# Attention's value product in high and low parts: the probabilities' low part on VectorE ahead of the next maximum

## What is computed

```
logits = einsum('bnqhgd,bnkhd->bnhgqk', qb, kb) * HEAD_DIM ** -0.5
logits = where(valid, logits, -1e30)
probs = softmax(concatenate([logits, sink_col], -1), -1)[..., :-1]
out = einsum('bnhgqk,bnkhd->bnqhgd', probs, vb)
```

## Time and profile before

| | us |
|---|---|
| median of 3 runs | 950.02 (949.94 to 950.05) |
| span of the profiled execution, first to last instruction | 948.2 |
| TensorE busy | 928.1 (98%) |
| TensorE weight loads | 800.5 (84%) |
| VectorE busy | 724.2 (76%) |
| ScalarE busy | 576.6 (61%) |

### The profile page before, as it was taken

The page is one execution under the profiler, slowest core; times in us unless marked ns, Lnnn a source line. Parts: engine busy times, 40 slices in busy tenths (PEclk is TensorE's granted clock), DMA queues, the critical chain, the costliest instruction groups (busy, mean ns, idle before and its releaser), DMA issues.

```text
span 948.2 us, 12500 instructions
## 1 busy us (share of the span) xinstructions
PE 928.1 (98%) x5068; PEld 800.5 (84%) x5068; DVE 724.2 (76%) x971; ACT 576.6 (61%) x730; POOL 1.4 (0%) x9
## 2 busy tenths in 40 slices
PE   4999999999999999999999999999999999999996
PEld 3898888988888888888889889888888888888885
DVE  5887898787867867767867688888878676866755
ACT  4578889764356644555345889887435564545540
POOL 0000000000000000000000000000000000000000
PEclk9999999999999999999999999999999999999998
DMA  9546444584485655566453544456756656555621
GB/s 330 159 160 200 135 156 156 185 303 166 156 266 183 200 195 178 194 201 207 157 162 122 204 159 157 132 179 192 261 177 216 229 185 203 189 179 196 202 90 45
DMA packets 118457, 174.62 MB, mean 184 GB/s; under 512 B 3968, under 2 KB 78976, under 8 KB 117888
## 3 DMA queue, kind: packets, MB, share of 16 engines
q1 hardware_dynamic: 118256, 173.79, 55.1%
q10 hardware_dynamic: 144, 0.03, 0.0%
HBM read 172.76 MB, written 1.05 MB: 183 GB/s over the span
## 4 chain that ended last, share of the span: by engine, by line
PE 97%; DVE 1%; DMA 1%; ACT 0%; SPq 0%; issue 0%; DVEq 0%
PE ring L541 16%; PE ring L543 16%; PE ring L542 16%; PE ring L594 9%; PE ring L590 9%; PE ring L593 5%; PE ring L591 5%; PE misc L543 5%; PE misc L541 5%; PE misc L542 4%; PE misc L771 2%; PE misc L809 1%; PE misc L829 1%; PE ring L714 1%; DMA sb_hb<-in_w_in_dram 1%; PE ring L725 1%
## 5 line engine op out<-in xcount | busy, mean ns | idle before, releaser
L1245 DVE TENSOR_TENSOR sb_w_lo<-sb_raw,sb_w_hi 128x2048 fp32r<-128x2048 f32 x138 | 294.7, 2148 | 67.5 <-ACT sb_w_hi L925 67.4
L925 ACT CAST sb_w_hi<-sb_raw 128x2048 fp32r<-128x2048 f32 x138 | 246.2, 1795 | 16.1 <-DMA sb_raw<-in_w_proj_rnn_dram 3.9
L541 PE MATMUL ring<-sb_w_hi,sb_x_both 128*128 128x512 f32 x272 | 108.1, 397 | 0.0
L594 PE MATMUL ring<-sb_x_both,sb_w_hi 128*128 128x512 f32 x272 | 107.6, 396 | 0.0
L590 PE MATMUL ring<-sb_x_both,sb_w_hi 128*128 128x512 f32 x272 | 107.5, 395 | 0.0
L543 PE MATMUL ring<-sb_w_hi,sb_x_both 128*128 128x512 f32 x272 | 106.1, 390 | 0.0
L542 PE MATMUL ring<-sb_w_lo,sb_x_both 128*128 128x512 f32 x272 | 106.0, 390 | 0.0
L593 PE MATMUL ring<-sb_x_both,sb_w_lo 128*128 128x256 f32 x272 | 75.7, 278 | 0.0
L591 PE MATMUL ring<-sb_x_both,sb_w_lo 128*128 128x256 f32 x272 | 75.4, 277 | 0.0
L541 PE MATMUL ring<-sb_x_both,sb_w_hi 128*128 128x256 f32 x256 | 73.0, 285 | 0.0
L543 PE MATMUL ring<-sb_x_both,sb_w_lo 128*128 128x256 f32 x256 | 72.4, 283 | 0.0
(11 more groups left out here) (223 smaller groups left out, 2085.8 us busy)
## 6 DMA issues: line engine op xcount, KB each, us to landing
sb_raw<-in_w_in_dram SPq DMA_DIRECT2D x40, 1024.0 KB, 5.2
sb_raw<-in_w_up_dram SPq DMA_DIRECT2D x34, 1024.0 KB, 5.2
sb_raw<-in_w_down_dram SPq DMA_DIRECT2D x18, 1024.0 KB, 4.9
sb_raw<-in_w_proj_attn_dram SPq DMA_DIRECT2D x8, 1024.0 KB, 5.0
sb_raw<-in_w_proj_rnn_dram SPq DMA_DIRECT2D x8, 1024.0 KB, 5.1
sb_hb<-in_w_up_dram SPq DMA_DIRECT2D x8, 1024.0 KB, 5.2
sb_raw<-in_w_out_dram SPq DMA_DIRECT2D x6, 1024.0 KB, 6.0
sb_raw<-in_w_ple_gate_dram SPq DMA_DIRECT2D x6, 1024.0 KB, 5.7
```

The source lines that it names most:

```text
L541: nc.tensor.matmul(dst, lhs[0], rhs[0], start=first, stop=False)
L594: last = nc.tensor.matmul(bank_of(*key), hi[:, cols], x_both[:, k + 1], start=False, stop=k + 2 == KT)
L925: nc.scalar.copy(hi_at[home][:, at], raw_at[home][:, at]).then_inc(s_hi_part, 1)
L1245: nc.vector.tensor_tensor(lo_at[home][:, 0:size], raw_at[home][:, 0:size], hi_at[home][:, 0:size].bitcast(F32), ALU.subtract).then_inc(s_s ...
```

## The change

The value product becomes three float32r products. For that both operands get a high and a low part:

- `v_hi` is a ScalarE copy of the values, once a layer, behind the last copy of turned keys in unit `ga0` (i = 2). `v_lo` is a VectorE subtraction, once a layer, in unit i = 3.
- `p_hi` is what `probs_back` writes, in the place of `pT`. `p_lo` is a VectorE subtraction that reads misc banks 2 and 3, in units 3 to 6, behind the taps and ahead of `softmax_max`.
- The new tiles lie on memory that is free by then: `v_hi` on the end of `qk`, `v_lo` on `v` itself, `p_lo` on the front of `qkT`, `p_hi` on `pT`. For the place of `p_lo`, round 0 also waits for the scores of round 1.
- `mix_values` waits for `v_lo` and `p_lo` and issues six float32r matmuls of 512 columns in the place of two float32 ones.

```
@@ -282,9 +282,12 @@
 
         h = sb("h", [P, TT, D])
         lnp = sb("lnp", [P, 2, D])
-        qk = sb("qk", [P, TT, QK_HEADS, HEAD_DIM])
-        v = sb("v", [P, TT, KV_HEADS, HEAD_DIM])
-        qkT = sb("qkT", [P, QK_HEADS, SEQ])
+        qk, at = sb_at("qk", [P, TT, QK_HEADS, HEAD_DIM])
+        v_hi = again("v_hi", [P, TT, KV_HEADS, HEAD_DIM], F32R, at + 4 * KT * SEQ)
+        v, at = sb_at("v", [P, TT, KV_HEADS, HEAD_DIM])
+        v_lo = again("v_lo", [P, TT, KV_HEADS, HEAD_DIM], F32R, at)
+        qkT, at = sb_at("qkT", [P, QK_HEADS, SEQ])
+        p_lo = again("p_lo", [P, TT, GROUP, P], F32R, at)
         yg = qk[:, :, :, :].rearrange("p t h d -> p (t h d)")[:, 0:KT * SEQ].rearrange(
             "p (k s) -> p k s", k=KT)
         hf = lnp[:, :, :].rearrange("p i (k s) -> p (i k) s", s=SEQ)
@@ -294,7 +297,8 @@
         ga = sb("ga", [P, TT, D])
         gr = xT[:, :, :].rearrange("p (t a) s -> p t (a s)", t=TT)
         soft = sb("soft", [P, GROUP, SEQ])
-        pT = sb("pT", [P, TT, GROUP, P])
+        pT, at = sb_at("pT", [P, TT, GROUP, P])
+        p_hi = again("p_hi", [P, TT, GROUP, P], F32R, at)
         scan_in, at = sb_at("scan_in", [P, 2, 4, SEQ])
         decay_a, root_m = scan_in[:, 0], scan_in[:, 1]
         scan_hi = again("scan_hi", [P, 2 * 4 * SEQ], F32R, at)
@@ -824,10 +831,11 @@
 
             def mix_values(l, r):
 
-                pe.wait_ge(s_probs_back, value("probs_back", l, r + 1))
+                pe.wait_ge(s_v_ready, value("v_ready", l, 1))
+                pe.wait_ge(s_probs_lo, value("probs_lo", l, r + 1))
                 for kb in range(TT):
-                    last = nc.tensor.matmul(misc[:, 2, :], v[:, kb, r // TT, :], pT[:, kb, :, :],
-                                            start=kb == 0, stop=kb == TT - 1)
+                    last = three(misc[:, 2, :], [x[:, kb, r // TT, :] for x in (v_hi, v_lo)],
+                                 [p_hi[:, kb, :, :], p_lo[:, kb, :, :]], kb == 0, kb == TT - 1)
                 last.then_inc(s_mixed, 1)
 
 
@@ -1027,7 +1035,7 @@
 
             def probs_back(l, r):
                 act.wait_ge(s_probs_turned, value("probs_turned", l, r + 1))
-                nc.scalar.copy(pT[:, :, :, :].rearrange("p a g t -> p (a g t)"),
+                nc.scalar.copy(p_hi[:, :, :, :].rearrange("p a g t -> p (a g t)"),
                                misc[:, 2:4, :].rearrange("p a n -> p (a n)")).then_inc(s_probs_back, 1)
 
             def attn_out(l, r):
@@ -1165,6 +1173,9 @@
                         conv_base(l, i + 2)
                     if name == "ga0":
                         qk_copies(l, [4])
+                        all_emptied(act, l, [("kv", t) for t in range(TT)])
+                        nc.scalar.copy(v_hi[:, :, :, :].rearrange("p t h d -> p (t h d)"),
+                                       v[:, :, :, :].rearrange("p t h d -> p (t h d)")).then_inc(s_v_hi, 1)
                     if 3 <= i <= 6:
                         probs_back(l, i - 3)
                     if i % 2 == 1:
@@ -1447,6 +1458,23 @@
                     last = nc.vector.tensor_scalar(soft[:, i, :], soft[:, i, :], sm[:, 5, i:i + 1], None, ALU.mult)
                 last.then_inc(s_probs, 1)
 
+            def v_low(l):
+                dve.wait_ge(s_v_hi, value("v_hi", l, 1))
+                nc.vector.tensor_tensor(v_lo[:, :, :, :].rearrange("p t h d -> p (t h d)"),
+                                        v[:, :, :, :].rearrange("p t h d -> p (t h d)"),
+                                        v_hi[:, :, :, :].rearrange("p t h d -> p (t h d)").bitcast(F32),
+                                        ALU.subtract).then_inc(s_v_ready, 1)
+
+            def probs_low(l, r):
+
+                dve.wait_ge(s_probs_back, value("probs_back", l, r + 1))
+                if r == 0:
+                    dve.wait_ge(s_scores, value("scores", l, TT))
+                nc.vector.tensor_tensor(p_lo[:, :, :, :].rearrange("p a g t -> p (a g t)"),
+                                        misc[:, 2:4, :].rearrange("p a n -> p (a n)"),
+                                        p_hi[:, :, :, :].rearrange("p a g t -> p (a g t)").bitcast(F32),
+                                        ALU.subtract).then_inc(s_probs_lo, 1)
+
             def attn_out(l, r):
                 g, b = divmod(r, TT)
                 at = (slice(None), slice(GROUP * g, GROUP * (g + 1)), slice(b * P, (b + 1) * P))
@@ -1630,6 +1658,10 @@
                     split_to(l, name, 1)
                     if i + 2 < 2 * RNN_BLOCKS:
                         conv(l, i + 2)
+                    if i == 3:
+                        v_low(l)
+                    if 3 <= i <= 6:
+                        probs_low(l, i - 3)
                     if 2 <= i <= 5:
                         softmax_max(l, i - 2)
                     if name == "kv":
```

More of the change, by code:

```diff
@@ L238 @@
 PER = dict(
-    ln_step=2 * TT * LN_STEPS, ln_norm=4 * TT, x_turned=3 * 4, x_hi=3 * 4, x_ready=3 * 4,
+    probs_lo=ROUNDS, v_ready=1, v_hi=1, ln_step=2 * TT * LN_STEPS, ln_norm=4 * TT, x_turned=3 * 4, x_hi=3 * 4, x_ready=3 * 4,
     rope_step=6, qk_turned=5, qk_ready=5,
@@ L353, in hybrid_encoder @@
         s_probs_back = sem("probs_back")
+        s_probs_lo = sem("probs_lo")
+        s_v_hi = sem("v_hi")
+        s_v_ready = sem("v_ready")
         s_mixed = sem("mixed")
```

## The result

The changed kernel takes 951.78 us (median of 16 runs, 951.58 to 953.16) against 950.16 us for the kernel before (16 runs, 949.93 to 951.33): ratio 1.0017, 95% interval 1.0010 to 1.0023, so 1.6 us slower. The forecast was 951.6.

The account below looks back on a forecast made before the run. TensorE, busy 928.1 of 948.2 us, was taken as the bound. Per layer 1.44 us saved against 2.25 waited gave +0.8, twice +1.6: median 951.6 us, 0.17% slower, range 949.4 to 954.0.

Parts of the forecast that it names:

- What TensorE saves: Value products in each round: six float32r at 0.227 us replace 1.72 us, saving 0.36 per round, 2.9 in all.
- Rival 3: Value products much cheaper than 0.227 us, at 0.12, but TensorE mostly waits for VectorE's slots: 949.8 us; chance 0.06.
- What VectorE pays: Added subtractions on VectorE: 1.73 us in round 0, 1.13 in other rounds; VectorE busy 11.1 us more.
- Round 1's wait: TensorE's value products in round 1 wait 0.71 us for VectorE's low part of the probabilities.
- The sum: Per layer 1.44 us saved and 2.25 waited: +0.8, twice +1.6, median 951.6 us.
- the case's own range: Forecast case with its bounds for saving, restart and turnings: +0.1 to +1.6 us a layer, 950.2 to 953.2 us.
- ScalarE's cover: ScalarE's copy of the values, near 0.6 us, costs nothing in the 2.74 us idle before the first exponentials.
- Rival 1: VectorE's slot comes 1.3 us earlier, so low parts are in time and the saving arrives whole: 947.1 us; chance 0.06.
- Rival 2: VectorE's backlog never drains, every round waits like round 0: 957.8 us, or half, 954 to 955; chance 0.14.
- Where the backlog drains: VectorE's backlog falls to some 1.5 us by round 2, in its 1.06 us idle before 146.57.
- Rival 4: TensorE's clock falls in the new waits, costing microseconds each time; chance 0.04 together with anything unseen.
- The cover of the weight splits: Weights' low parts are made three pieces ahead on VectorE, so a backlog up to 2.6 us there costs nothing.

Follow-up runs that it names:

- e1: The changed kernel with six float32r products on the high parts alone, no low parts made or waited for: 947.43 us, ratio 0.997.
- e2: The changed kernel with VectorE's subtractions kept, but the value product float32 and waiting only for ScalarE's copy: 952.57 us, ratio 1.0027.
- e4: The changed kernel with both low-part subtractions moved ahead of the convolution's six taps on VectorE: 951.82 us, ratio 1.0018.
- e8: The changed kernel with the subtractions behind the next round's maximum instead of ahead of it: 964.29 us, ratio 1.0143.
- e7: The changed kernel with values' low part earlier, probabilities' ahead of the taps, and two weight splits moved behind the attention output's low part: 949.83 us.
- e10: e7 with round 3's probabilities' low part also moved ahead of a weight split: 948.76 us, ratio 0.9986.
- e9: The changed kernel with values' low part earlier, probabilities' low part in two halves, first three products behind the first half: 951.07 us, ratio 1.0010.

## Why the prediction was right

The mechanism is the one forecast: TensorE waits for VectorE's low part in rounds 0 and 1, is late enough in rounds 2 and 3 not to wait, and what it loses is a little more than what the products save. Round by round in layer 0. Lags are counted from the first turning, which is 0.28 us later than before.

| step | forecast | measured |
|---|---|---|
| round 0: wait | 1.34 | 1.35 |
| lag at the next turning | 1.08 | 129.91 - 128.50 - 0.28 = 1.13 |
| round 1: wait | 0.71 | 0.51 |
| lag at round 2 | 1.43 | 156.38 - 154.71 - 0.28 = 1.39 |
| rounds 2 and 3: wait | none | none |
| lag behind round 3 | 0.8 | 174.19 - 173.10 - 0.28 = 0.81 |

(173.10 is the first gate product of the kernel before, taken from its record's end, 173.38, less 0.28.)

- **What TensorE saves.** 0.227 a product was right: 0.23 in the rows after, 0.34 us a round in e1 against 0.36 forecast. Rival 3, the cheap product, is out.
- **What VectorE pays.** The low part ends and the products start where they were put: 119.77 - 0.28 = 119.49, forecast 119.48. Durations were 0.69 and 1.22 us, as in the earlier trace rows. Reading PSUM costs the subtraction nothing: e2's, which reads SBUF alone, takes 1.22 too. In busy time VectorE gets 9.4 us and not the 11.1 that were to show it. That number added durations; by the pitches, 2 x (0.60 + 4 x 1.13), it is 10.2, and the rest is near an estimate from the rows: in four places a layer a gap of before is filled now, and two records overlap there by 0.09.
- **Round 1's wait** is a size that was off, by 0.20, without harm to the sum. TensorE came 0.1 later (the restart's extra 0.07, left out of my sum, and the turning), VectorE was 0.08 earlier, since the gap of 0.46 was worth 0.54. A wait that one engine's lateness shortens corrects such errors: what is over-counted before it is under-counted in it.
- **The sum** of a layer, +0.8, was met within 0.03, and part of that is luck: the waits came to 1.86 us where 2.05 were forecast, which is 0.19 less; two restarts of 0.07, in no term of the sum, and a saving of 1.37 (e1) instead of 1.44 make it up by 0.21. The low end of the case's own range, +0.1 a layer, was added up wrongly, by terms that the next wait partly takes back. Gone through round by round with the same values it is +0.4, an estimate.
- **ScalarE's cover** held. The values' copy takes 0.62 us and the idle time ahead of the exponentials falls from 2.74 to 2.22.
- **Rival 1** is out where the waits are: in e1 TensorE needs less, and VectorE's slot still stands at 117.47 and 135.67 on the clock of before (118.51 and 136.71, less 1.04), against 117.51 and 135.71. In round 2 its mechanism is real: the slot comes 0.72 earlier (153.26 - 1.04 = 152.22 against 152.94), but no product waits there.
- **Rival 2** is out, but narrowly, and which way it would fall was not forecast. The exponentials of round 1 start at 140.69, and the maximum that they need ends at 140.49 + 0.16 = 140.65. In e4 they are held by 0.51 us, and yet the waits don't grow from round to round there.
- **Where the backlog drains** was named wrongly, though the size was right. The prediction put its fall to 1.5 at the gap of 1.06 before 146.57, which is still 1.03 in the change (row of 148.29 in VectorE's timeline above). VectorE's lateness is 138.31 - 135.71 - 0.28 = 2.32 at round 1's mask add and 142.77 - 141.02 - 0.28 = 1.47 where the softmax sums begin. What it used up is the gap ahead of that step in the kernel before:

```profile
141.02 0.16 DVE L1442 TENSOR_TENSOR sb_sm<-sb_sm 128x4 f32<-128x4 f32 x1 [0.77 <-ACT sb_sm L1026]
```

- **Rival 4** is out here (granted clock 1.00 through the wait of 1.35) and true in e8.
- **The cover of the weight splits** was told as a flat three pieces. It held in the change and did not in e7, where the split that was moved was waited for.

The small loss has the cause given: work for VectorE in the one stretch where its list runs close to TensorE's. The products' gain is real (e1), the price is 4.3 us (951.78 less 950.16, and the 2.69 of e1), and most of it depends on VectorE's order: the work of e10 is that of the change, and it pays 1.3.

## What to carry to other kernels

Before giving work to an engine with idle time, find the steps at which the bounding engine arrives together with it; its busy share (76% here) says nothing about them. Fill the gaps in which it waits for a third engine, and move work with distant due times behind what is due. A wait removed at one step comes back at the next (e4, e9) unless the late engine's list is itself shortened or reordered up to that step, so count to the end of the stretch, not to the first wait.

## What was not expected of the hardware

- TensorE's wait of 3.4 us, once in each layer of e8, cost about 4.0 us beside itself over the two layers: the granted clock fell to 1.2 GHz within it in layer 0 and just behind it in layer 1, and the work until about 127.7 us, in layer 1 until about 595.3, ran at that. Waits of 1.35 us (the change) and of 1.7 us (e8, round 2, products 0.23 apart behind it) left it at 2.4 GHz. The Trainium skill, "TensorE: Matmul & The Clock Gate", section "HAM oscillation — how this bites in real kernels", tells of this pattern, work that starts slow behind a wait for data; this trace agrees (0.43 us between products instead of 0.23).
- The first of a group of 512-column products behind a wait costs 0.30 us instead of 0.23. Behind e8's long wait it costs 0.56 in layer 0, where the others at the lower clock cost 0.43, and 0.44 in layer 1.
